# Root mean square norms of a decoder step: statistics as columns of 128 tokens, spread to rows by a product with the identity

## The chip, the cores and the metric

One core of a Trainium2 chip runs the whole step as one launch. The metric is the device time in microseconds (us), median of three runs.

## The reference

Two layers of a decoder, width 1024, over 512 prompt tokens and 8 sample tokens (520 columns, one per token). Layer 0 is a state space layer (S5), layer 1 attends with decay to a paged cache (FoX). Both attend to a memory, and each has a sandwich norm and a feed-forward part:

```python
def rmsnorm(x, g):
    y = xf * lax.rsqrt(jnp.mean(xf * xf, axis=-1, keepdims=True) + EPS)
    return y.astype(x.dtype) * g
...
        x = x + rmsnorm(o, p['norm_mix_post'][l])
        f, cp = conv_ffn(rmsnorm(x, p['norm_ffn_pre'][l]), p['w_up'][l], ...)
        x = x + rmsnorm(f, p['norm_ffn_post'][l])
```

So between two big products there are always two norms in a row: that of the product's output (post), which is added to the residual stream `x`, and that of the new `x` (pre), whose factor each token of the next product is multiplied by.

## The kernel before

Activations lie transposed: the 128 partitions are features, the 1024 features are 8 blocks `k`, and the 520 tokens are the columns, in two halves `HALF` of 264 and 256. A product runs in panels of 128 output features. A panel takes three matmuls for each `k` and half, of split operands: `x_hi` by `w_hi`, `x_lo` by `w_hi`, `x_hi` by `w_lo`. The weights' parts `w_hi` are made by ScalarE (`hi`), `w_lo` by GpSimd or VectorE (`lo`), and each stage waits for the one before by semaphores.

At four places a product is followed by two norms (`post_norm` on VectorE, `post` on ScalarE, `last_pair` and `first_pair` on TensorE): behind `wout0` (300 us), `down01` (708 us), `wout1` (1078 us), and `down11` at the end (1484 us), where only the post norm follows. The order of the work there is written out by hand, instruction by instruction, with constants that say at which step `i` or `k` something stands (`LAST_READ`, `ROOT_1`, `HI_NEXT`, `ROOT_PRE`, `RECIP_PRE`, `LO_FIRST`, `LO_NEXT`).

- `last_pair` computes the last two panels (6 and 7) by halves: half 0 of both, then half 1 of both. In the midst of half 1 of panel 6, `post_stats(stats, 0)` sums the squares of half 0 over the features: three float32 matmuls with the stationary matrix `meanw` (128x128, each entry 1/1024), so that every partition of the result holds each token's mean square. A float32 matmul is two instructions on the engine.
- ScalarE takes the root (`root_half`, 264 or 256 columns on all partitions, into `sd`), VectorE the reciprocal (`reciprocal_half`, into `rstd`).
- VectorE then goes through 16 steps (half, k): scale `y` by gain and `rstd` (L1738), add it to `x` (L1744), and two steps behind make `x_lo` (L1251). ScalarE makes `x_hi` and the squares of `x` from each new `x`. Two `w_lo` (L1208) of the next phase stand in this order too, at steps 1 and 11.
- `first_pair` computes the next phase's first two panels by halves (half 0 of both, half 1 of both), each `k` as soon as its `x_lo` is there. Behind k = 2 of its first quarter stand `post_stats(before, 1)` and the first sums of `x_stats` (`add`), one matmul with `meanw` for each block of squares; they give the pre norm's mean squares. Its reciprocals write `rstd`, by which the next phase's readers (`uc`, `qh`) multiply each panel.

The mean squares lie in a ring of four PSUM banks (`misc`), each freed by the engine that reads it.

## Time and profile before

| | |
|---|---|
| median of 3 runs | 1521.39 us (1520.93 to 1525.54) |
| span of the profiled execution | 1519.0 us |
| TensorE busy | 1413.4 us, 93% |
| VectorE busy | 976.7 us, 64% |
| ScalarE, GpSimd busy | 576.7, 638.5 us |
| mean granted TensorE clock | 0.971 |

The profile states the span from the first to the last instruction of one execution; the time of that same execution is not stated beside it. The median is 2.4 us above the span, which is what lies around it. In timelines the first two numbers are start and duration in us; PE is TensorE, DVE VectorE, ACT ScalarE, and an arrow "<-" in brackets names what ended the idle time before the instruction. Matmuls are pipelined, so that in a string of them the distance of starts, not the duration, is the cost of one.

### The profile page before, as it was taken

The numbers are of one execution on the slowest core, as the hardware profiler recorded it, in microseconds if no ns is written. First come the engines' busy times: TensorE is split into PE (matmuls) and PEld (weight loads), VectorE is DVE, ScalarE is ACT, GpSimd is POOL, SyncE is SP. The second block draws the span as 40 slices with busy tenths as digits, with TensorE's granted clock in tenths as the row PEclk, the third lists the DMA queues.
The fourth block names the chain that finished last, engine by engine and source line by source line (L and its number), as shares of the span: only waits on it lengthen the run. The fifth ranks groups of instructions, "written<-read, shape, count | busy, mean of one in ns | idle before, by whom it ended". The sixth has DMA issues, their size and how long they took to land.

```text
span 1519.0 us, 32537 instructions
## 1 busy us (share of the span) xinstructions
PE 1413.4 (93%) x12097; PEld 1313.9 (86%) x12097; DVE 976.7 (64%) x1658; ACT 576.7 (38%) x1019; POOL 638.5 (42%) x420
## 2 busy tenths in 40 slices
PE   6986978989999999999799989999989999999997
PEld 6984758979999999999699966657889999999997
DVE  5769967576773167765748688753677761376755
ACT  4544354344432133422415235432454431234323
POOL 1586422304444334433177888402223443344430
PEclk9998789989999999999999999999999999999999
DMA  5344364213333232332145769995213233233321
GB/s 173 114 117 79 63 169 123 83 44 85 99 94 98 77 97 83 102 98 75 45 121 164 226 175 308 331 340 157 69 57 97 84 103 90 83 91 88 104 83 62
DMA packets 289082, 180.47 MB, mean 119 GB/s; under 512 B 54248, under 2 KB 274572, under 8 KB 288924
## 3 DMA queue, kind: packets, MB, share of 16 engines
q1 hardware_dynamic: 288412, 179.07, 40.9%
q8 instruction: 61, 1.00, 0.3%
q14 instruction: 33, 0.27, 0.1%
q10 hardware_dynamic: 576, 0.13, 0.0%
HBM read 167.10 MB, written 10.63 MB: 117 GB/s over the span
## 4 chain that ended last, share of the span: by engine, by line
PE 70%; DVE 14%; issue 8%; ACT 2%; SPq 2%; DMA 1%; POOL 1%; DVEq 0%; ACTq 0%; POOLq 0%
PE big L2649 58%; PE big L2715 3%; PE misc L2800 2%; DVE tmp L1261 2%; PE big L2746 2%; DVE y L1738 1%; DVE rstd L1219 1%; DVE x L1744 1%; DVE w_lo L1208 1%; DVE x_lo L1251 1%; SPq L597 1%; PE misc L2770 1%; ACT yc L2506 1%; DVE cp L1261 1%; ACT w_hi L2144 1%
## 5 line engine op out<-in xcount | busy, mean ns | idle before, releaser
L949 POOL TENSOR_TENSOR w_lo<-raw,w_hi 128x1024 fp32r<-128x1024 f32 (+2 forms) x153 | 393.8, 2574 | 708.9 <-ACT w_hi L2144 548.4
L2144 ACT ACTIVATE w_hi<-raw 128x1024 fp32r<-128x1024 f32 (+2 forms) x179 | 198.5, 1109 | 582.1 <-PE big L2649 539.0
L2649 PE MATMUL big<-x_hi,w_hi 128*128 128x264 f32 x1984 | 406.7, 287 | 8.4 <-DVE uc L1827 2.8
L2649 PE MATMUL big<-x_hi,w_lo 128*128 128x264 f32 x1984 | 400.8, 283 | 0.0
L2649 PE MATMUL big<-x_lo,w_hi 128*128 128x264 f32 x1984 | 398.8, 283 | 0.0
L2649 PEld LDWEIGHTS big<-x_hi,w_hi 128*128 128x128 f32 x1984 | 305.9, 189 | 13.1 <-issue 4.7
L2649 PEld LDWEIGHTS big<-x_lo,w_hi 128*128 128x128 f32 x1984 | 305.6, 189 | 0.0
L2649 PEld LDWEIGHTS big<-x_hi,w_lo 128*128 128x128 f32 x1984 | 305.3, 189 | 0.0
L1831 DVE SCALAR_TENSOR_TENSOR yc<-uc,convw,yc 128x512 f32<-128x512 f32 x88 | 136.7, 1554 | 113.2 <-ACT yc L2506 113.2
L2649 PE MATMUL big<-h_hi,w_hi 128*128 128x264 f32 x616 | 125.1, 284 | 6.3 <-DVE h_lo L1846 6.3
L2649 PE MATMUL big<-h_hi,w_lo 128*128 128x264 f32 x616 | 123.9, 282 | 0.0
L2649 PE MATMUL big<-h_lo,w_hi 128*128 128x264 f32 x616 | 123.9, 282 | 0.0
L2649 PEld LDWEIGHTS big<-h_hi,w_hi 128*128 128x128 f32 x616 | 94.1, 188 | 7.4 <-DVE h_lo L1846 7.1
L2649 PEld LDWEIGHTS big<-h_lo,w_hi 128*128 128x128 f32 x616 | 94.4, 188 | 0.0
L2649 PEld LDWEIGHTS big<-h_hi,w_lo 128*128 128x128 f32 x616 | 94.4, 188 | 0.0
L1859 DVE COPY y<-big 128x264 f32 (+1 forms) x32 | 12.2, 424 | 102.6 <-PE big L2649 102.6
L1093 POOL TENSOR_TENSOR areas<-areas,qb 128x768 f32<-128x768 f32 x41 | 74.6, 1830 | 7.0 <-DMA areas<-in_cache_k 6.2
L1836 DVE SCALAR_TENSOR_TENSOR yc<-uc,convw,yc 128x512 f32<-128x512 f32 x88 | 66.2, 752 | 12.7 <-DVE yc L1834 0.2
L2506 ACT ACTIVATE yc<-uc,convw 128x520 f32<-128x520 f32 x88 | 72.3, 821 | 1.1
L1201 DVE TENSOR_TENSOR sumsq<-sumsq,sq 128x520 f32<-128x520 f32 x20 | 52.5, 2627 | 11.7 <-ACT sq L2461 9.9
L2746 PE MATMUL big<-x_hi,w_hi 128*128 128x264 f32 (+1 forms) x96 | 38.4, 400 | 17.8 <-DVE x_lo L1251 10.4
L1219 DVE RECIPROCAL rstd<-sd 128x264 f32<-128x264 f32 (+1 forms) x16 | 28.3, 1773 | 31.5 <-ACT sd L2177 31.5
(434 smaller groups left out, 2330.8 us busy)
## 6 DMA issues: line engine op xcount, KB each, us to landing
raw<-in_w_up SPq DMA_DIRECT2D x88, 512.0 KB, 3.9
raw<-in_w_down SPq DMA_DIRECT2D x32, 704.0 KB, 4.7
areas<-in_cache_k SPq DMA_DIRECT2D x41, 384.0 KB, 4.5
areas<-in_cache_v SPq DMA_DIRECT2D x41, 384.0 KB, 4.7
raw<-in_w_in SPq DMA_DIRECT2D x16, 512.0 KB, 4.2
raw<-in_w_out SPq DMA_DIRECT2D x16, 512.0 KB, 4.2
raw<-in_w_kv SPq DMA_DIRECT2D x12, 512.0 KB, 4.6
spare<-in_cache_k SPq DMA_DIRECT2D x12, 384.0 KB, 4.5
```

The costliest lines, as they stand in the source:

```text
L949: pool.tensor_tensor(w_lo[slot][:, 0:kb, :], raw[slot][:, 0:kb, :], w_hi[slot][:, 0:kb, :].bitcast(F32), ALU.subtract).then_inc(lo_made, 1)
L1093: own.tell(pool.tensor_tensor(p, p, qb[b % 2][:].rearrange("p (a d) -> p a d", a=2), ALU.mult), s_("k_product"), n + 1)
L1201: ins = V.tensor_tensor(sumsq[:], sumsq[:], sq[:, m % 2, :], ALU.add)
L1219: tell(V.reciprocal(rstd[:, c0:c1], sd[:, c0:c1]), s_("rstd_ready"), nstd[0])
L1261: do(V.tensor_tensor(o, a_, b_, op))
L1831: st(V.scalar_tensor_tensor(yy[:, 0:T], uu[:, 1:1 + T], w_[1], yy[:, 0:T], ALU.mult, ALU.add))
L1836: st(V.scalar_tensor_tensor(yy[:, 0:T], uu[:, 0:T], w_[0], yy[:, 0:T], ALU.mult, ALU.add))
L2144: A.activation(w_hi[slot][:, 0:kb, :], raw[slot][:, 0:kb, :], ACT.Copy).then_inc(hi_made, 1)
L2506: A.activation(yy[:], uu[:, 2:2 + NT], ACT.Identity, bias=convw[:, 1 - l, bass.ds(it + (f * KH + half * KF + 132), 1)], scale=convw[:, 1 - ...
L2649: ins = pe.matmul(big[2 * slot + b_][:, 0:c1 - c0], w[slot][:, k, :], r[:, c0:c1], start=(k == 0 and n_ == 0), stop=(k == kb - 1 and n_ == 2))
L2715: return pe.matmul(big[2 * slot + b_][:, 0:c1 - c0], w[slot][:, k, :], r[:, c0:c1], start=(k == 0 and n_ == 0), stop=(k == kb - 1 and n_ = ...
L2746: ins = pe.matmul(big[2 * slot + b_][:, 0:c1 - c0], w[slot][:, k, :], r[:, k, c0:c1], start=(k == 0 and n_ == 0), stop=(k == KD - 1 and n_ ...
```

## The change

In `post_norm`, `post`, `last_pair` and `first_pair` the statistics change their shape. The squares are now the stationary operand, 128 tokens at a time, and one column of `meanw` is the moving one. The result is a column: a token on each partition. Half 0 (264 tokens) takes three such blocks (the third overlaps the second, and only its last 8 tokens are used), half 1 (256) takes two. Root and reciprocal run on 128x3 or 128x2 elements. Then `spread_row` turns them to rows again: the reciprocals' column, repeated 128 times, is stationary and the identity moves, so that each partition of the result, in the same PSUM bank from column 8 on, holds each token's factor. VectorE reads the post norm's factors straight from there; ScalarE copies the pre norm's into `rstd`.

The constants move the roots and reciprocals to other steps, and `read_half` of panel 6 goes behind the first `y`. The norms of `x0` and of the memory stay as they were. Three start-up semaphores become one. The diff, cut:

```diff
@@ -148,6 +148,20 @@
...
+def stat_blocks(n):
+
+    c0, c1 = HALF[n]
+    full_ = [(c0 + P * j, P * j, 0) for j in range((c1 - c0) // P)]
+    over = (c1 - c0) % P
+    return full_ + ([(c1 - P, c1 - c0 - over, P - over)] if over else [])
+
+
+ROW = 8
+
+
 def by_half():
 
     return enumerate((n, k) for n in range(2) for k in range(KD))
@@ -195,8 +209,8 @@
 KV_HI = 4
-ROOT_1, HI_NEXT, ROOT_PRE, RECIP_PRE = 6, 8, 10, 13
-LO_FIRST, LO_NEXT = 1, 11
+RECIP_1, ROOT_1, HI_NEXT, ROOT_PRE, RECIP_PRE, ROWS_PRE = 7, 4, 8, 13, 15, 15
+LO_FIRST, LO_NEXT, LAST_READ_END = 1, 11, 5
 K_FIRST = (2, 3)
@@ -582,6 +596,16 @@
 
+        def stat_cols_at(i, n):
+
+            c = 8 * (i % 4)
+            w = len(stat_blocks(n))
+            return sd[:, c:c + w], sd[:, 32 + c:32 + c + w]
+
+        def stat_row(job):
+
+            return bank(job)[:, ROW:ROW + HALF[job[2]][1] - HALF[job[2]][0]]
+
         def gain(name, k, l=0):
@@ -1218,6 +1242,25 @@
 
+            ncol = [0]
+
+            def reciprocal_cols(n):
+
+                root, recip = stat_cols_at(ncol[0], n)
+                ncol[0] += 1
+                dve.wait_ge(s_("root_cols"), ncol[0])
+                tell(V.reciprocal(recip, root), s_("rstd_ready"), 3 + ncol[0])
+
+            def row_spread(i):
+
+                dve.wait_ge(s_("row_spread"), i)
+
+            def rows_read(name):
+
+                for n in range(2):
+                    _, _, read, before = place(("ms", name, n))
+                    dve.wait_ge(read, before + 1)
+
             def reciprocal_halves(name):
...
@@ -1723,24 +1766,31 @@
                 sync()
-                reciprocal_half(stats, 0)
-                sync()
-                read_half(ph, 6, 1, add)
+                last_read = LAST_READ if nxt is not None else LAST_READ_END
+                reciprocal_cols(0)
+                first = ncol[0]
+                row_spread(first)
                 steps = [k for _, k in by_half()]
...
                 for i in range(2 * KD + 2):
+                    if i == (RECIP_1 if nxt is not None else KD):
+                        reciprocal_cols(1)
                     if i == KD:
-                        reciprocal_half(stats, 1)
-                        sync()
+                        row_spread(first + 1)
                     if i < 2 * KD:
...
                         c = slice(*HALF[n])
-                        tell(V.scalar_tensor_tensor(y[:, k, c], y[:, k, c], gain(name, k, l), rstd[:, c], ALU.mult,
-                                                    ALU.mult), s_("y_scaled"), done + i + 1)
+                        tell(V.scalar_tensor_tensor(y[:, k, c], y[:, k, c], gain(name, k, l),
+                                                    stat_row(("ms", stats, n)), ALU.mult, ALU.mult),
+                             s_("y_scaled"), done + i + 1)
+                    if i == 0:
+                        read_half(ph, 6, 1, add)
                     if 1 <= i <= 2 * KD:
...
                         dve.wait_ge(s_("y_scaled"), done + i)
+                        if k == KD - 1:
+                            dve.sem_inc(place(("ms", stats, n))[2], 1)
                         tell(V.tensor_tensor(x[:, k, c], x[:, k, c], y[:, k, c], ALU.add), s_("x_updated"), done + i)
@@ -1750,14 +1800,14 @@
                         lo(PH[ph][2] + 9)
-                    if i == LAST_READ:
+                    if i == last_read:
                         read_half(ph, 7, 1, add)
...
                     if nxt is not None and i == RECIP_PRE:
-                        reciprocal_half(stat_name[1], 0)
+                        reciprocal_cols(0)
                 if nxt is not None:
-                    reciprocal_half(stat_name[1], 1)
-                    sync()
+                    reciprocal_cols(1)
+                    rows_read(stat_name[1])
 
@@ -2176,6 +2226,21 @@
 
+            ncol = [0]
+
+            def root_cols(name, n):
+
+                job, (root, _) = ("ms", name, n), stat_cols_at(ncol[0], n)
+                ncol[0] += 1
+                full(act, job)
+                tell(A.activation(root, bank(job)[:, 0:len(stat_blocks(n))], ACT.Sqrt, bias=eps[:, 0:1]),
+                     s_("root_cols"), ncol[0])
+
+            def copy_row(name, n, i):
+
+                act.wait_ge(s_("row_spread"), i)
+                freed(own, A.activation(rstd[:, slice(*HALF[n])], stat_row(("ms", name, n)), ACT.Copy), ("ms", name, n))
+
             def root_halves(name):
...
@@ -2465,7 +2530,7 @@
                 square_half(ph, 7, 0)
-                root_half(name, 0)
+                root_cols(name, 0)
                 if (ph, name) != ("down11", "d1"):
@@ -2480,14 +2545,17 @@
                         square_half(ph, 7, 1)
-                    elif i == ROOT_1:
-                        root_half(stats, 1)
-                    elif i == HI_NEXT:
+                    if i == ROOT_1:
+                        root_cols(stats, 1)
+                    if i == HI_NEXT:
                         hi(PH[after][0], base + n + 1)
-                    elif i == ROOT_PRE:
-                        root_half(name, 0)
+                    if i == ROOT_PRE:
+                        root_cols(name, 0)
+                    if i == ROWS_PRE:
+                        copy_row(name, 0, ncol[0])
+                root_cols(name, 1)
                 hi(KD, base + n + 2)
-                root_half(name, 1)
+                copy_row(name, 1, ncol[0])
                 ny[0] += 1
...
@@ -2695,11 +2763,27 @@
                     pe.wait_ge(s_("sq_used"), 2 + 6 * npost[0])
-                o, (c0, c1) = take(("ms", name, n)), HALF[n]
+                o = take(("ms", name, n))
                 pe.wait_ge(s_("sq_last"), 4 * npost[0] - 2 + 2 * n)
-                pe.matmul(o[:, 0:c1 - c0], meanw[:], sumsq[:, c0:c1], start=True, stop=False)
-                pe.matmul(o[:, 0:c1 - c0], meanw[:], sq[:, 0, c0:c1], start=False, stop=False)
-                give(pe.matmul(o[:, 0:c1 - c0], meanw[:], sq[:, 1, c0:c1], start=False, stop=True), ("ms", name, n))
+                for j, (at, _, _) in enumerate(stat_blocks(n)):
+                    t = slice(at, at + P)
+                    pe.matmul(o[:, j:j + 1], sumsq[:, t], meanw[:, 0:1], start=True, stop=False)
+                    pe.matmul(o[:, j:j + 1], sq[:, 0, t], meanw[:, 0:1], start=False, stop=False)
+                    ins = pe.matmul(o[:, j:j + 1], sq[:, 1, t], meanw[:, 0:1], start=False, stop=True)
+                give(ins, ("ms", name, n))
+
+            nrow = [0]
+
+            def spread_row(name, n):
+
+                i, o = nrow[0], bank(("ms", name, n))
+                nrow[0] += 1
+                pe.wait_ge(s_("rstd_ready"), 3 + i + 1)
+                _, recip = stat_cols_at(i, n)
+                for j, (_, at, skip) in enumerate(stat_blocks(n)):
+                    ins = pe.matmul(o[:, ROW + at:ROW + at + P - skip], recip[:, j:j + 1].to_broadcast([P, P]),
+                                    ident[:, skip:P], start=True, stop=True)
+                ins.then_inc(s_("row_spread"), 1)
 
@@ -2723,6 +2807,8 @@
                                 post_stats(stats, 0)
+                        if b_ == 1 and p_ == 0:
+                            spread_row(stats, 0)
                         if b_ == 0:
@@ -2753,6 +2839,12 @@
                                 add(b_, KD - 1)
+                            if b_ == 0 and p_ == 0 and k == 5:
+                                spread_row(before, 1)
+                            elif b_ == 1 and p_ == 0 and k == 2:
+                                spread_row(name, 0)
+                            elif b_ == 1 and p_ == 1 and k == 5:
+                                spread_row(name, 1)
                         if b_:
@@ -2763,11 +2855,12 @@
                 def add(n, k):
-                    c0, c1 = HALF[n]
                     if k == 0:
...
                     pe.wait_ge(s_("xsq_made"), done + KD * n + k + 1)
-                    ins = pe.matmul(o[n][:, 0:c1 - c0], meanw[:], y[:, k, c0:c1], start=(k == 0), stop=(k == KD - 1))
+                    for j, (at, _, _) in enumerate(stat_blocks(n)):
+                        ins = pe.matmul(o[n][:, j:j + 1], y[:, k, at:at + P], meanw[:, 0:1], start=(k == j == 0),
+                                        stop=(k == KD - 1 and at + P == HALF[n][1]))
                     if k == KD - 1:
...
@@ -3377,6 +3470,7 @@
             post_stats("d1", 1)
+            spread_row("d1", 1)
             for c, a_ in TURNED_OUT:
```

In the rows that follow, `misc` is the bank of statistics, `big` that of a panel. On TensorE, in `last_pair("wout0")`, half 1 of panel 6, before:

```order
L2715 MATMUL big<-x_lo,w_hi 128x256
L2700 MATMUL misc<-sumsq,meanw 128x264
L2701 MATMUL misc<-sq,meanw 128x264
L2702 MATMUL misc<-sq,meanw 128x264
L2715 MATMUL big<-x_hi,w_hi 128x256
L2715 MATMUL big<-x_lo,w_hi 128x256
L2715 MATMUL big<-x_hi,w_hi 128x256
```

and now, from the last three column products of the statistics on:

```order
L2770 MATMUL misc<-meanw,sumsq 128x1
L2771 MATMUL misc<-meanw,sq 128x1
L2772 MATMUL misc<-meanw,sq 128x1
L2799 MATMUL big<-x_hi,w_hi 128x256
L2799 MATMUL big<-x_lo,w_hi 128x256
L2799 MATMUL big<-x_hi,w_hi 128x256
L2799 MATMUL big<-x_lo,w_hi 128x256
L2799 MATMUL big<-x_hi,w_hi 128x256
L2799 MATMUL big<-x_lo,w_hi 128x256
L2784 MATMUL misc<-ident,sd 128x128 x2
L2784 MATMUL misc<-ident,sd 128x8
```

Three products have become nine (six of them stand ahead of these rows), and the spread of half 0 stands ahead of the panel's `w_lo` products.

On TensorE, in the `first_pair` behind it, from the post norm's statistics of half 1 (behind k = 2) on, before:

```order
L2700 MATMUL misc<-sumsq,meanw 128x256
L2701 MATMUL misc<-sq,meanw 128x256
L2702 MATMUL misc<-sq,meanw 128x256
L2770 MATMUL misc<-y,meanw 128x264 x2
L2746 MATMUL big<-x_hi,w_hi 128x264
L2746 MATMUL big<-x_lo,w_hi 128x264
L2746 MATMUL big<-x_hi,w_lo 128x264
L2770 MATMUL misc<-y,meanw 128x264
```

and now, from the first of the six statistics products on:

```order
L2770 MATMUL misc<-meanw,sumsq 128x1
L2771 MATMUL misc<-meanw,sq 128x1
L2772 MATMUL misc<-meanw,sq 128x1
L2770 MATMUL misc<-meanw,sumsq 128x1
L2771 MATMUL misc<-meanw,sq 128x1
L2772 MATMUL misc<-meanw,sq 128x1
L2862 MATMUL misc<-meanw,y 128x1 x6
L2832 MATMUL big<-x_hi,w_hi 128x264
L2832 MATMUL big<-x_lo,w_hi 128x264
L2832 MATMUL big<-x_hi,w_lo 128x264
L2862 MATMUL misc<-meanw,y 128x1 x3
```

and, behind k = 5:

```order
L2832 MATMUL big<-x_hi,w_lo 128x264
L2862 MATMUL misc<-meanw,y 128x1 x3
L2784 MATMUL misc<-ident,sd 128x128 x2
L2832 MATMUL big<-x_hi,w_hi 128x264
L2832 MATMUL big<-x_lo,w_hi 128x264
```

Each sum over a block of `x` has become three products, and the row that VectorE waits for comes from the spread (`L2784`) behind k = 5.

On VectorE, in `post_norm`, around step 8, where half 1 begins, before:

```order
L1744 TENSOR_TENSOR x<-x,y 128x264
L1251 SCALAR_TENSOR_TENSOR x_lo<-x,gains,x_hi 128x264
L1219 RECIPROCAL rstd<-sd 128x256
L1738 SCALAR_TENSOR_TENSOR y<-y,gains,rstd 128x256
L1744 TENSOR_TENSOR x<-x,y 128x264
L1251 SCALAR_TENSOR_TENSOR x_lo<-x,gains,x_hi 128x264
```

and now:

```order
L1252 RECIPROCAL sd<-sd 128x2
L1783 SCALAR_TENSOR_TENSOR y<-y,gains,misc 128x264
L1794 TENSOR_TENSOR x<-x,y 128x264
L1294 SCALAR_TENSOR_TENSOR x_lo<-x,gains,x_hi 128x264
L1783 SCALAR_TENSOR_TENSOR y<-y,gains,misc 128x256
L1794 TENSOR_TENSOR x<-x,y 128x264
```

The reciprocal of 256 columns has become one of 2, one step earlier, and the scaling reads its factors from `misc`.

## Rows read from the trace of the kernel before

**Rows 1.** The page: busy time by engine, and the chain that ended last.

```profile
PE 1413.4 (93%) x12097; PEld 1313.9 (86%) x12097; DVE 976.7 (64%) x1658; ACT 576.7 (38%) x1019; POOL 638.5 (42%) x420
...
PE 70%; DVE 14%; issue 8%; ACT 2%; SPq 2%; DMA 1%; POOL 1%; DVEq 0%; ACTq 0%; POOLq 0%
```

**Rows 2.** The page, costliest groups: the reciprocals of the norms.

```profile
L1219 DVE RECIPROCAL rstd<-sd 128x264 f32<-128x264 f32 (+1 forms) x16 | 28.3, 1773 | 31.5 <-ACT sd L2177 31.5
```

**Rows 3.** Timeline of VectorE behind `wout1`: start us, us, engine, line, what.

```profile
1089.40 0.89 DVE L1738 SCALAR_TENSOR_TENSOR y<-y,gains,rstd 128x264 f32<-128x264 f32 x2
...
1090.55 1.22 DVE L1208 TENSOR_TENSOR w_lo<-raw,w_hi 128x1024 fp32r<-128x1024 f32 x1
...
1099.99 1.75 DVE L1219 RECIPROCAL rstd<-sd 128x256 f32<-128x256 f32 x1 [0.85 <-ACT sd L2177]
1101.78 0.48 DVE L1738 SCALAR_TENSOR_TENSOR y<-y,gains,rstd 128x256 f32<-128x256 f32 x1
```

**Rows 4.** Timeline of TensorE over the same stretch.

```profile
1084.96 0.69 PE L2700 MATMUL misc<-sumsq,meanw 128*128 128x264 f32 x2
...
1095.74 0.42 PE L2746 MATMUL big<-x_hi,w_hi 128*128 128x264 f32 x1 [0.53 <-DVE x_lo L1251]
...
1096.40 1.05 PE L2700 MATMUL misc<-sumsq,meanw 128*128 128x256 f32 x2
...
1107.64 0.39 PE L2746 MATMUL big<-x_hi,w_hi 128*128 128x264 f32 x1 [2.37 <-DVE w_lo L1208]
...
1111.82 0.59 PE L2770 MATMUL misc<-y,meanw 128*128 128x256 f32 x2
...
1120.16 0.28 PE L2746 MATMUL big<-x_hi,w_lo 128*128 128x256 f32 x1
...
1121.85 0.51 PE L2649 MATMUL big<-x_hi,w_hi 128*128 128x264 f32 x2 [1.41 <-DVE uc L1827]
```

**Rows 5.** Timeline of TensorE: small matmuls with 64 or 128 stationary columns.

```profile
11.25 1.02 PE L2800 MATMUL misc<-ident,xs_tok 8*128 8x8 f32 x8
12.20 6.21 PE L2800 MATMUL misc<-ident,x_tok 128*128 128x128 f32 x32
...
949.24 0.69 PE L3032 MATMUL misc<-y,probT 128*64 128x64 f32 x16
949.85 0.83 PE L3314 MATMUL misc<-rowsel,rstd 128*128 128x2 f32 x6
950.54 0.68 PE L2998 MATMUL big<-kh,qh 128*128 128x512 f32 x1
...
1503.72 1.04 PE L2800 MATMUL misc<-ident,x 128*128 128x128 f32 x8
```

**Rows 6.** Two small operations, by line: nanoseconds min/median/max.

```profile
L1946 DVE TENSOR_TENSOR qs<-big,rstd x6: 167/168/168, 756.4 to 783.6; 128x8 f32<-128x8 f32 x6
...
L2464 ACT ACTIVATE root_warm<-eps x4: 203/203/203, 302.0 to 1486.9; 128x1 f32<-128x1 f32 x4
```

**Rows 7.** Timelines behind `down01`: VectorE, then TensorE.

```profile
722.80 1.22 DVE L1208 TENSOR_TENSOR w_lo<-raw,w_hi 128x1024 fp32r<-128x1024 f32 x1
...
756.68 0.48 PE L2649 MATMUL big<-x_hi,w_hi 128*128 128x264 f32 x2 [2.38 <-DVE qs L1946]
```

**Rows 8.** Timelines at the end: TensorE, then VectorE.

```profile
1493.41 0.61 PE L2700 MATMUL misc<-sumsq,meanw 128*128 128x264 f32 x2
...
1497.84 0.89 DVE L1738 SCALAR_TENSOR_TENSOR y<-y,gains,rstd 128x264 f32<-128x264 f32 x2
...
1507.32 0.48 DVE L1738 SCALAR_TENSOR_TENSOR y<-y,gains,rstd 128x256 f32<-128x256 f32 x1
```

**Rows 9.** Windows: busy us of PE, PEld, DVE, ACT, POOL; granted clock, DMA share, GB/s.

```profile
1096.00:1099.40 3.40, 3.40 (x11) 2.77 (x11) 3.14 (x9) 2.43 (x7) 0.00 (x0) 0.50 0.00 0
...
328.00:334.80 6.80, 6.13 (x26) 5.93 (x27) 5.03 (x10) 1.89 (x5) 0.00 (x0) 0.50 0.31 80
...
860.00:890.00 30.00, 29.38 (x233) 27.93 (x232) 26.04 (x41) 5.15 (x7) 24.33 (x13) 1.00 0.49 151
```

More of the change, by code:

```diff
@@ L148 @@
 TURNED_OUT = [(c, a) for cs in ((0, 1), (2, 3, 4)) for a in range(2) for c in cs]
+PARAMS = {"lrow": 1, "lam": 2, "gains": 3}
+def stat_blocks(n):
[4 more added lines that the diff above has]
+ROW = 8
 def by_half():
@@ L1523, in _ @@
                              dtrow[:].unsqueeze(2).to_broadcast([PAIRS, 2, STATE])))
-            mark(s_("lrow_ready"))
+            mark(s_("params_ready"))
             evac(("lam",), lam[:, 0:96], bank(("lam",))[:, 0:96])
-            mark(s_("lam_ready"))
+            mark(s_("params_ready"))
             s5_rates()
             evac(("rows",), gains[:], bank(("rows",))[:, 0:100])
-            mark(s_("gains_ready"))
+            mark(s_("params_ready"))
             evac(("xsT",), x[:, :, T:NT], bank(("xsT",))[:, 0:KD * NB].rearrange("p (k b) -> p k b", b=NB))
@@ L2223, in mem_turned @@
                 mark(s_("memtok_ready"))
-            act.wait_ge(s_("lam_ready"), 1)
+            act.wait_ge(s_("params_ready"), PARAMS["lam"])
             tell(A.activation(lam[:, 64:64 + PAIRS], lam[:, 64:64 + PAIRS], ACT.Exp), s_("s5_act"), 1)
@@ L2228, in _ @@
             do(A.activation(root_warm[:], eps[:], ACT.Sqrt))
-            act.wait_ge(s_("gains_ready"), 1)
+            act.wait_ge(s_("params_ready"), PARAMS["gains"])
             for k in range(KD):
@@ L2598, in _ @@
             square_half("down11", 7, 1)
-            root_half("d1", 1)
+            root_cols("d1", 1)
             for c, a_ in TURNED_OUT:
@@ L2802, in _ @@
             pe.wait_ge(s_("consts"), 1)
-            pe.wait_ge(s_("lrow_ready"), 1)
+            pe.wait_ge(s_("params_ready"), PARAMS["lrow"])
             pe.wait_ge(s_("lam_in"), 48)
```

## The prediction

> **What bounds the kernel now.** I read the page first: TensorE is busy 93% of the span and holds 70% of the chain that ended last, VectorE 14% [rows 1]. Where TensorE runs panels back to back a norm costs nothing, so only the four places where a product meets two norms can move the time, and they must be read one by one in the timelines of VectorE and TensorE. There the 16 reciprocals of 264 or 256 columns take 1.77 us each [rows 2]; two are those of `x0`, which stay, so 14 become small.
>
> The place behind `wout1` stands for `wout0` too. It has three links. (A) The statistics of half 0 start at 1084.96 [rows 4], the first `y` at 1089.40 [rows 3]; then `w_lo` at 1090.55 waits for what ScalarE makes once panel 6 is done. (B) TensorE takes k = 2 of the next panel at 1095.74, then the statistics of half 1 and the sums of `x` [rows 4]; VectorE waits 0.85 us for the root, spends 1.75 us on the reciprocal and starts half 1 at 1101.78 [rows 3]. (C) From there VectorE's order is fixed up to the second `w_lo`, which lets TensorE go on at 1107.64. From 1107.64 to 1120.28 (the last start plus one distance of 0.12) TensorE never waits: it, not VectorE, is the bound [rows 4]. (D) The next panel starts at 1121.85, 1.57 us later, behind the reciprocal and the first readings.
>
> So a faster VectorE helps in A, B and the tail D, while each instruction that is added on TensorE costs in B and C.
>
> **What an instruction with one moving column costs.** The trace has none, but it has its neighbours. Six float32 matmuls with 128 stationary and 2 moving columns start at 949.85 and the next matmul at 950.54: 0.115 us each; the eight with 8 moving columns go from 11.25 to 12.20: 0.119 each [rows 5]. Moving almost nothing, they cost what the stationary load costs. The lower bound is 16 matmuls with 64 stationary columns in 0.61 us, 0.038 each, so 0.076 for twice the columns if they scale [rows 5]; the upper one is 0.22 to 0.24, what a float32 instruction with 256 moving columns takes now (two between 1111.82 and the next sum about 0.79 later, of which three matmuls take 0.36: 0.43 for the pair) [rows 4]. I take 0.115, since number and shape of the stationary columns are the same. An instruction of the spread moves 128 columns as the transposes do, eight in 1.04 us, or 0.11 each [rows 5]; its block of 8 columns takes 0.115.
>
> The Trainium skill, "TensorE: Matmul & The Clock Gate", section "LDWEIGHTS (loading the stationary operand)", gives the number of columns over 1.2, so 107 ns for 128, whatever the moving side. The rows agree within 10%; by its figure the loss below would be 0.6 us smaller at each of the three places. [...]
>
> **Term A.** Statistics: 3 products with 3 blocks are 18 instructions, 2.2 us with the last one's end, where 6 took about 1.6 with it. Root and reciprocal on three columns: a 128x1 root takes 0.20 us and a 128x8 operation on VectorE 0.17 [rows 6]; I take 0.20 and 0.15 (bounds 0.06 and 0.3). TensorE has 6 panel matmuls (0.7 us) to do in the meantime, so this costs it no wait. Spread: 4 by 0.11 and 2 by 0.115, 0.83 with its end. With about 0.08 for each of four signals the first `y` starts 3.7 us behind the statistics, not 4.4: 0.7 earlier. But panel 6 ends 0.75 (18 x 0.115 less the 1.32 of now) plus 0.67 (spread) later, 1.4 us; ScalarE's `w_hi` and then `w_lo` follow it. They had about 1.2 us to spare, so the first `x_lo` comes 0.2 us **later**. Behind `down01`, where `w_lo` starts at 722.80 [rows 7] close behind its `w_hi`, 1.0 of the 1.4 is left, and the reading of panel 7 waits another 0.4: 1.4 us later.
>
> **Term B.** From k = 2 on TensorE must do: 3 matmuls (0.36), 12 instructions of statistics and 12 of the first two sums (2.76), then for k = 3, 4, 5 each 3 matmuls and 6 column instructions (3 x 1.05 = 3.15), then the spread of 4 (0.60 with its end) and a signal (0.08): 6.95 us until VectorE may start half 1. Now it is 1101.78 - 1095.74 = 6.04. VectorE's saved 1.75 + 0.85 us turn into a wait for a spread that stands three blocks further down TensorE's queue: **+0.9 us**. Root and reciprocal are hidden by those blocks; at 0.3 instead of 0.15 nothing changes.
>
> **Term C.** The stretch that TensorE bounds gets: the last sum of half 0, 6 x 0.115 against 0.44, +0.25; eight sums of half 1, 4 x 0.115 against 0.43, +0.2; the two spreads of the pre norm, 0.67 and 0.44. Together **+1.6 us**, with no cover.
>
> **Term D.** ScalarE copies the second row (a row root takes 0.48 us today, and I take that) while TensorE does its last 6 matmuls (0.71). The copy is over about when TensorE is; then come 0.37 for the `uc` start-up and 0.82 for the readings: 1.25 instead of 1.57, **-0.3**. Behind `down01` it is the same (next panel at 756.68 [rows 7]).
>
> **The end.** Statistics at 1493.41, first `y` at 1497.84; half 1 from 1507.32 [rows 8]. Half 0 starts 0.3 earlier; half 1 waits for root, reciprocal and spread behind 12 column instructions whose squares come 1.4 us later, and starts near 1506.7. From there all is as now: **-0.6**.
>
> **Sum.** `wout0` and `wout1`: 0.2 + 0.9 + 1.6 - 0.3 = 2.4 each; `down01`: 1.4 + 0.9 + 1.6 - 0.3 = 3.6; the end -0.6. Together +7.8 on a span of 1519.0, so 1526.8, and with the 2.4 that lie around it 1529.2: 1529 us, 0.5% slower.
>
> **Rivals.**
> *The load hides* (faster). If a column instruction costs no more than its share of the 64-column row, 0.038, B's 42 column instructions shrink by 3.2 us, C's 38 by 2.9. VectorE's chain then bounds B, and of its 2.6 us of wait and reciprocal about 2.3 are gained; C is paid back. With D this is near -3 us at three places, -0.6 at the end: 1512. It decides at about 0.09 us for an instruction, where B and C come to nothing. For it speaks that TensorE's loads overlap running matmuls now; against it that in both strings of small matmuls they do not get below 0.115. 0.16.
> *Half way* (within 0.3%). At 0.076, B and C shrink by 1.6 and 1.5: -0.7 at two places, +0.5, -0.6: 1520. Or the two early losses are made good while cache pages stream: but right ahead of that stage, 860 to 890 us, the DMA share is 0.49 and TensorE is busy 29.4 of 30 us [rows 9], so the stage waits for the product and starts later with it. 0.18.
> *The clock* (slower still). Behind `wout1` the granted clock was 0.50 in 1096.0 to 1099.4, just the stretch of B, and behind `wout0` 0.50 in 328.0 to 334.8, in C, where TensorE's panels took twice the time [rows 9]. Both came behind waits of TensorE of 2 us. Such waits stay, and much of the work between becomes loads; if the level stays at 1.2 GHz for one such stretch of 6.8 us more at each of three places, at some 3 us each, the time is 1538. 0.16.
> *The forecast*: 0.50.
>
> **How the numbers follow.** 0.3% (4.6 us) is about what a measurement of this kernel can tell from no change. The forecast and the clock are slower: 0.65 with the forecast's edge at +5 given to no change; half way is the same: 0.19; faster 0.16. The range reaches to the half-way case and most of the clock case, 1518 to 1537; outside lie the rest of the clock case and the hidden load.
>
> **What would show it.** Right: in strings of `128x1` matmuls starts 0.11 to 0.12 apart; VectorE idle 2 to 3 us ahead of step 8, ended by the spread; 14 to 14.5 us for the stretch from the first panel's second quarter to the end; 128x3 reciprocals under 0.2 us; the four places +2.4, +3.6, +2.4, -0.6. Wrong: starts 0.08 or less apart, or no wait ahead of step 8, or a clock at half over the whole place.

## The result

| | before | changed |
|---|---|---|
| median of 4 runs | 1523.47 us (1520.93 to 1530.24) | 1560.89 us (1557.74 to 1561.76) |
| span of the profiled execution | 1519.0 us | 1555.8 us |
| mean granted TensorE clock | 0.971 | 0.951 |

The ratio is 1.0232, 95% interval 1.0211 to 1.0254: the change costs 37 us. The forecast was 1529 with a range up to 1537, so it had the sign and missed the size by 32 us. Both profiled executions are the fastest of their four (1520.93 and 1557.74 us); where a median execution spends the 2.5 and 3.2 us more, no trace shows.

### The profile page after: what moved, and what is told of

Same layout as the page of the kernel before. It is cut to its first block, busy times and chain, and to the rows that moved or that the text cites. A ratio compares the mean times of both kernels' runs of the same rounds, so it can differ in the third digit from the quotient of the medians.

```text
span 1555.8 us, 33107 instructions
## 1 busy us (share of the span) xinstructions
PE 1458.4 (94%) x12383; PEld 1363.3 (88%) x12383; DVE 954.8 (61%) x1658; ACT 576.0 (37%) x1025; POOL 638.3 (41%) x420
## 4 chain that ended last, share of the span: by engine, by line
PE 77%; DVE 13%; issue 3%; ACT 2%; DMA 1%; SPq 1%; POOL 1%; DVEq 0%; ACTq 0%; POOLq 0%
PE big L2717 57%; PE big L2799 3%; PE big L2832 3%; PE misc L2893 2%; PE misc L2862 2%; DVE tmp L1304 2%; PE misc L3392 1%; DVE sc L1980 1%; DVE y L1783 1%; DVE w_lo L1232 1%; DVE x L1794 1%; DVE ast L1530 1%; SPq L621 1%; PE misc L3125 1%; DVE x_lo L1294 1%
## 5 line engine op out<-in xcount | busy, mean ns | idle before, releaser
L1909 DVE COPY y<-big 128x264 f32 (+1 forms) x32 | 12.2, 424 | 102.3 <-PE big L2717 102.3
L2254 ACT ACTIVATE x_hi<-x,gains 128x264 fp32r<-128x264 f32 (+2 forms) x64 | 35.3, 560 | 47.3 <-DVE x L1794 39.7
L2832 PE MATMUL big<-x_hi,w_hi 128*128 128x264 f32 (+1 forms) x96 | 38.7, 404 | 12.1 <-DVE x_lo L1294 10.5
```

Source lines behind the costliest of these rows:

```text
L2254: ins = A.activation(o, src, ACT.Copy, scale=1.0 if g is None else g)
L2832: ins = pe.matmul(big[2 * slot + b_][:, 0:c1 - c0], w[slot][:, k, :], r[:, k, c0:c1], start=(k == 0 and n_ == 0), stop=(k == KD - 1 and n_ ...
```

## The profile after

The page of the changed kernel, busy time and chain (before: [rows 1]):

```profile
PE 1458.4 (94%) x12383; PEld 1363.3 (88%) x12383; DVE 954.8 (61%) x1658; ACT 576.0 (37%) x1025; POOL 638.3 (41%) x420
...
PE 77%; DVE 13%; issue 3%; ACT 2%; DMA 1%; SPq 1%; POOL 1%; DVEq 0%; ACTq 0%; POOLq 0%
```

VectorE has become 22 us less busy, TensorE 45 us more. The costly groups, each shape by itself (busy, mean ns of one, idle time ahead):

```profile
L2862 PEld LDWEIGHTS misc<-meanw,y 128*128 128x128 f32 x240 | 46.0, 276 | 0.0
...
L1783 DVE SCALAR_TENSOR_TENSOR y<-y,gains,misc 128x256 f32<-128x256 f32 x32 | 15.1, 473 | 24.7 <-PE misc L2784 24.7
```

VectorE's idle time ahead of the reciprocals, ended by the root, was 31.5 us [rows 2] and is 43.0 ahead of the fourteen small ones (L1252). A second wait has come beside it: 24.7 us ahead of half 1's scaling, ended by the spread (L2784).

Where the 36.8 us of span went is read from windows, each from the start of half 0's statistics to the next phase's first panel (behind `wout0`, `down01`, `wout1`), and to the end. These windows are called places from here on. Columns: length, then busy time of PE, PEld, DVE, ACT and POOL, the granted clock (PEclk; 1.00 is the full 2.4 GHz, 0.50 the half), DMA share and GB/s. Before:

```profile
305.99:345.63 39.64, 32.94 (x179) 28.98 (x179) 29.44 (x60) 18.24 (x42) 2.39 (x1) 0.83 0.12 30
717.23:756.68 39.45, 30.85 (x197) 27.59 (x195) 30.67 (x62) 19.17 (x42) 3.56 (x2) 0.96 0.13 36
1084.96:1121.84 36.88, 29.18 (x180) 25.53 (x178) 29.44 (x60) 18.23 (x42) 2.40 (x1) 0.95 0.11 31
1493.41:1519.00 25.59, 16.67 (x108) 14.51 (x106) 16.32 (x36) 7.64 (x14) 0.00 (x0) 0.87 0.23 84
...
756.68:1084.96 328.28, 312.45 (x2750) 253.20 (x2751) 212.94 (x366) 119.00 (x253) 193.05 (x102) 0.99 0.70 218
```

Changed, with a stretch inside each place:

```profile
306.07:353.60 47.53, 42.15 (x265) 40.96 (x265) 23.10 (x60) 18.20 (x45) 2.36 (x1) 0.75 0.09 24
724.95:774.34 49.39, 43.69 (x282) 42.72 (x281) 24.33 (x62) 19.02 (x44) 3.07 (x2) 0.76 0.07 22
1108.37:1156.03 47.66, 42.15 (x266) 40.96 (x265) 23.13 (x60) 17.98 (x44) 2.36 (x1) 0.75 0.08 23
1527.31:1555.80 28.49, 19.27 (x136) 17.94 (x134) 13.12 (x36) 7.31 (x14) 0.00 (x0) 0.88 0.21 76
...
318.00:341.80 23.80, 21.94 (x100) 21.56 (x100) 14.20 (x37) 10.66 (x27) 0.00 (x0) 0.50 0.09 24
...
738.00:761.60 23.60, 21.74 (x100) 21.36 (x100) 14.22 (x37) 10.66 (x27) 0.00 (x0) 0.50 0.08 23
...
1120.20:1144.00 23.80, 21.94 (x100) 21.56 (x101) 14.31 (x37) 10.75 (x27) 0.00 (x0) 0.50 0.08 23
...
774.34:1108.37 334.03, 317.31 (x2751) 255.29 (x2751) 213.74 (x366) 119.19 (x253) 192.77 (x102) 0.97 0.68 215
```

The three places cost +7.9, +9.9 and +10.8, the end +2.9: 31.5 us together. The attention stage between the second and third place took 5.8 more. That is not shown to be the change's: no kernel here changes anything in that stage, and in the fourteen profiled executions it takes from 328.1 us (`post_rows`) to 334.5 (`more12`), so that it was the execution before that was short. Against the forecast's +7.8 on the span, the 36.8 are 23.7 too much in the four places and 5.8 in this stage. In each place the granted clock (from here on: the level) is at half, 1.2 GHz, for 23.6 us and more on end, though TensorE is busy 92% of that time.

The timeline of TensorE behind `wout1` (before: [rows 4]):

```profile
1108.37 0.35 PE L2770 MATMUL misc<-meanw,sumsq 128*128 128x1 f32 x2
...
1110.37 0.36 PE L2799 MATMUL big<-x_hi,w_hi 128*128 128x256 f32 x1
...
1119.39 0.39 PE L2832 MATMUL big<-x_hi,w_hi 128*128 128x264 f32 x1 [0.52 <-DVE x_lo L1294]
...
1122.10 2.70 PE L2862 MATMUL misc<-meanw,y 128*128 128x1 f32 x12
1124.66 0.57 PE L2832 MATMUL big<-x_hi,w_hi 128*128 128x264 f32 x1
...
1130.48 1.20 PE L2784 MATMUL misc<-ident,sd 128*128 128x128 f32 x4
...
1137.58 0.59 PE L2832 MATMUL big<-x_hi,w_hi 128*128 128x264 f32 x1 [0.54 <-DVE w_lo L1232]
...
1154.40 0.28 PE L2832 MATMUL big<-x_hi,w_lo 128*128 128x256 f32 x1
1156.02 0.51 PE L2717 MATMUL big<-x_hi,w_hi 128*128 128x264 f32 x2 [1.35 <-DVE uc L1877]
```

and of VectorE (before: [rows 3]):

```profile
1112.01 0.49 DVE L1783 SCALAR_TENSOR_TENSOR y<-y,gains,misc 128x264 f32<-128x264 f32 x1 [0.93 <-PE misc L2784]
...
1122.57 0.17 DVE L1252 RECIPROCAL sd<-sd 128x2 f32<-128x2 f32 x1 [0.94 <-ACT sd L2236]
...
1131.72 0.48 DVE L1783 SCALAR_TENSOR_TENSOR y<-y,gains,misc 128x256 f32<-128x256 f32 x1 [7.85 <-PE misc L2784]
```

Up to k = 2 the clock is full and everything is as forecast: 18 column instructions take 2.00 us (1108.37 to 1110.37), 0.111 each, and the first `y` starts 3.64 us behind the statistics. Then twelve take 2.56 us (1122.10 to 1124.66), **0.213 each**, VectorE waits 7.85 us where the forecast had 2 to 3, and the panels behind run at 0.22 a matmul until 1144. The fall itself, at 1120.1, is not new: it comes behind three waits of TensorE for `x_lo` (0.87, 0.92, 0.52 us), and in the kernel before the level was also down behind such waits, up to 1099.4 [rows 9]. What is new is that it stays down.

## Experiments

Two theories. **The clock**: the column products let the granted clock fall and keep it down; that is what the forecast lacks. **The count** (with the queue): the number of loads (each matmul has a load of its stationary operand, PE and PEld both x12383), and the spread's place in TensorE's queue, cost more than thought; the level is a bystander. What the runs gave, places as windows from half 0's statistics to the next panel, with their mean granted clock:

| run | median, ratio to before (95%) | `wout0` | `down01` | `wout1` |
|---|---|---|---|---|
| before | 1523 to 1525 | 39.6 (0.83) | 39.5 (0.96) | 36.9 (0.95) |
| changed | 1560.89, 1.0232 (1.0211 to 1.0254) | 47.5 (0.75) | 49.4 (0.76) | 47.7 (0.75) |
| wide64 | 1557.51, 1.0201 (1.0164 to 1.0238) | 47.6 (0.75) | 49.5 (0.76) | 46.2 (0.78) |
| wide128 | 1538.62, 1.0083 (1.0056 to 1.0110) | 42.6 (0.92) | 41.1 (1.00) | 41.0 (0.96) |
| pre_rows | 1537.74, 1.0078 (1.0048 to 1.0108) | 40.1 (0.91) | 45.0 (0.85) | 43.3 (0.84) |
| post_rows | 1534.49, 1.0069 (1.0044 to 1.0094) | 44.5 (0.73) | 42.1 (0.84) | 42.3 (0.80) |
| fill | 1549.49, 1.0159 (1.0126 to 1.0192) | 44.3 (0.81) | 47.7 (0.79) | 44.4 (0.85) |
| late_sums | 1542.90, 1.0113 (1.0068 to 1.0159) | 44.7 (0.77) | 44.8 (0.81) | 44.6 (0.77) |
| more12 | 1525.32, 0.9998 (0.9985 to 1.0012) | 38.0 (0.87) | 37.9 (1.00) | 38.0 (0.87) |
| fill_before | 1525.68, 1.0001 (0.9984 to 1.0018) | 37.7 (0.95) | 38.7 (0.96) | 37.7 (0.95) |
| more40 | 1559.01, 1.0228 (1.0208 to 1.0247) | 50.3 (0.80) | 49.6 (0.83) | 50.3 (0.80) |
| more40_wide | 1537.67, 1.0093 (1.0070 to 1.0115) | 42.6 (0.92) | 43.1 (0.96) | 42.4 (0.92) |
| late_wide | 1526.39, 1.0006 (0.9989 to 1.0023) | 37.4 (0.95) | 39.2 (0.96) | 36.2 (1.00) |
| mix | 1519.43, 0.9971 (0.9954 to 0.9987) | 36.0 (0.95) | 36.7 (1.00) | 35.1 (1.00) |

**64 moving columns for 1.** In both kinds of column product:

```diff
-ROW = 8
+ROW = 0
+WIDE, SUMS = 64, 272
...
-                    pe.matmul(o[:, j:j + 1], sumsq[:, t], meanw[:, 0:1], start=True, stop=False)
+                    pe.matmul(o[:, SUMS + WIDE * j:SUMS + WIDE * j + WIDE], sumsq[:, t], meanw[:, 0:WIDE], start=True, stop=False)
```

> The changed kernel with one difference: in the column products (statistics and sums of x) 64 equal columns of the mean matrix move instead of 1, so each takes the same stationary load but TensorE's array works through 64 columns; ScalarE takes every 64th column of the result. Clock theory (with one moving column the array does so little that the granted clock drops to 1.2 GHz and stays there for 23.9 us at each norm, and that is what costs 8 to 10 us a place): the stretches at half clock at the three norms shrink to 7 us or less, 128x64 instructions start 0.11 to 0.12 apart there, and the time is 1526 to 1535 us. Count theory (the time goes into the number of loads and the place of the spread in TensorE's queue, whatever the level): no change or slightly slower, 1560 to 1568 us. Waits theory (TensorE's waits ahead of k = 0 to 2 drop the level, not the columns): still 23.9 us at half at each place, 1560 us.

The clock theory missed: nothing changes, and each place still has 20 to 24 us at half (0.75 to 0.78 of its window). The run left the count theory and the waits standing.

**Which columns.** `pre_rows` has the old `add` of `x_stats`, with row root and row reciprocal; `post_rows` the old `post_stats` and scaling by `rstd`, with no spread between the halves. `pre_rows` on TensorE:

```diff
-                    for j, (at, _, _) in enumerate(stat_blocks(n)):
-                        ins = pe.matmul(o[n][:, j:j + 1], y[:, k, at:at + P], meanw[:, 0:1], start=(k == j == 0),
-                                        stop=(k == KD - 1 and at + P == HALF[n][1]))
+                    c0, c1 = HALF[n]
+                    ins = pe.matmul(o[n][:, 0:c1 - c0], meanw[:], y[:, k, c0:c1], start=(k == 0), stop=(k == KD - 1))
```

> The changed kernel with the sums of x (pre norms) made as rows again, root and reciprocal of 264 and 256 columns; only the post norms' statistics go through columns and the spread. 15 of the 55 column products of a place stay. Clock theory: a group of 12 instructions behind k = 2 and six panels' blocks behind it do not hold the level down; half clock 3 to 10 us a place, total 1522 to 1532. Count theory: what is lost goes by the number of column instructions, 30 of 110 and 6 of 11 spread products stay, so about a third of the 37 us is left: 1534 to 1540.

> The changed kernel with the post norms' statistics as rows again; the sums of x stay 40 column products a place, with the spread and the copies into rows behind them. VectorE has its reciprocals of 264 and 256 columns back ahead of each half, and no spread stands between the halves. Clock theory: the column sums alone keep the level at half for 15 us or more a place, total 1542 to 1560. Count theory: two thirds of the loss stay, 1545 to 1550, with the level at half no longer than before the change (3 to 7 us). The clock rows decide, not the time.

`pre_rows` ended on the count side: the level comes back sooner than in the changed kernel, but half 1's spread still stands behind k = 5, and VectorE waits 4.41 us for it at `wout0`. `post_rows` is below both ranges, with the level down for longer than before the change (0.73, 0.84 and 0.80 for 0.83, 0.96 and 0.95; at `wout0` 23.7 us on end): the sums of `x` alone do that, where VectorE waits for no spread of a post norm. So the level's length, which was to decide, is on the clock's side, and the time on neither: 10 us are lost, where the clock theory had 18 and more.

**24 column instructions into the kernel before.**

```diff
                                 add(0, 0)
                                 add(0, 1)
+                                add.more(12, 1)
...
+                def more(count, width):
+                    for _ in range(count):
+                        pe.matmul(o[0][:, 384:384 + width], meanw[:], meanw[:, 0:width], start=False, stop=False)
```

> The kernel before, with 12 column products (24 instructions, mean matrix stationary, one moving column, results unread) behind the first two sums of x at k = 2 of the first panel, at each of the three places. Count theory: 24 x 0.115 = 2.8 us, nearly all under the 2.4 us that TensorE waits for the second w_lo and the 0.4 before it: within 0.5 us a place, 1523 to 1526 us. Clock theory: the level falls to half there and stays, the panels behind take twice the time: 3 to 7 us a place, 1532 to 1545 us, with stretches at half of 10 us or more.

No loss: the 2.8 us lie in TensorE's wait for `w_lo`. A few column products cost nothing where TensorE has slack; here the count theory had the time. The level does fall behind them at `wout0`, but for 3.4 us only (0.50 in 326.4 to 329.8), and is full behind that.

**TensorE kept at work in its waits.** `fill` and `fill_before` put products of 256 moving columns into them:

```diff
+                            if b_ == 0 and p_ == 0 and k < 3:
+                                fill(slot, (7, 7, 4)[k])
                             if p_ == 0:
                                 x_split(KD * b_ + k)
```

> The changed kernel with TensorE kept at work where it waited: ahead of k = 0, 1, 2 of each first panel 7, 7 and 4 products of 256 moving columns (0.12 us each, results overwritten later) in place of waits of 0.87, 0.92 and 0.52 us, and 10 behind the spread of half 1 for the wait of 1.32. All column products stay. Clock theory (the waits let the level fall, the column products behind them keep it at half): the level stays full through k = 2 and the columns behind it, VectorE's wait ahead of step 8 is 2 to 4 us and not 7.9, and the place costs the forecast's +2.4: 1526 to 1534 us. If the columns alone bring the level down: 1545 to 1560. Count theory: 1560 to 1565, since work is only added.

> The kernel before, with TensorE kept at work in its waits as in the run above (7, 7, 4 products ahead of k = 0 to 2, and 18 ahead of the second panel, for 2.37 us). Clock theory: the half-clock stretches at wout0 (two of 6.8 us), down01 and wout1 (3.4 each) go; only C at wout0 is bound by TensorE in one of them, so about 3 us are won there and none elsewhere: 1519 to 1523 against 1524. Otherwise: 1524 to 1526, the stretches as before.

The timeline of TensorE in `fill`, behind `wout0`:

```profile
320.80 1.48 PE L2871 MATMUL misc<-meanw,y 128*128 128x1 f32 x12
322.14 0.37 PE L2840 MATMUL big<-x_hi,w_hi 128*128 128x264 f32 x1
...
322.58 0.81 PE L2871 MATMUL misc<-meanw,y 128*128 128x1 f32 x6
323.25 0.57 PE L2840 MATMUL big<-x_hi,w_hi 128*128 128x264 f32 x1
...
324.06 1.27 PE L2871 MATMUL misc<-meanw,y 128*128 128x1 f32 x6
```

and in windows:

```profile
318.50:322.80 4.30, 4.25 (x38) 4.04 (x36) 4.07 (x12) 3.38 (x10) 0.00 (x0) 1.00 0.01 3
323.10:340.00 16.90, 16.81 (x78) 16.72 (x79) 11.45 (x29) 8.20 (x20) 0.00 (x0) 0.50 0.13 34
```

With one wait of 0.15 us left ahead of them the first 24 instructions of statistics and sums run at full clock, 12 in 1.34 us (320.80 to 322.14), six more in 0.67, and then the level falls all the same, at 323, in the midst of a TensorE that has stood still for no more than that. So in the changed kernel the waits bring the fall forward and are not needed for it. In the kernel before they do matter: behind `wout1` k = 2 and the statistics now run at full level (1100.42 to 1105), where they ran at half, and the half level comes behind a wait that was not filled, 2.08 us ahead of the matmul at 1107.75. Filling won nothing there, against what the clock theory had promised: 1.0001.

**128 moving columns.** Only a line differs from `wide64`:

```diff
-WIDE, SUMS = 64, 272
+WIDE, SUMS = 128, 0
```

> As the run with 64 moving columns, with 128, as many as are loaded. With 64 the stretches at half did not shorten (23.9, 23.9, 20.5 us). If the share of time in which the array has columns to work on decides, they shorten to 7 to 14 us and the time is 1535 to 1550; if it is the stationary load in between that holds the level down whatever moves, they stay at 20 to 24 us: 1556 to 1562.

The windows of its places:

```profile
306.90:349.49 42.59, 35.51 (x266) 34.19 (x265) 23.11 (x60) 18.33 (x45) 2.36 (x1) 0.92 0.11 27
720.75:761.86 41.11, 33.80 (x282) 32.80 (x281) 24.33 (x62) 19.03 (x44) 3.08 (x2) 1.00 0.09 27
1096.12:1137.15 41.03, 33.91 (x266) 32.58 (x265) 23.13 (x60) 18.00 (x44) 2.36 (x1) 0.96 0.09 27
```

And at `wout0` from the statistics of half 1 on:

```profile
318.40:321.70 3.30, 3.30 (x20) 3.30 (x19) 2.20 (x7) 1.48 (x6) 0.00 (x0) 0.55 0.00 0
321.90:330.00 8.10, 6.78 (x57) 6.56 (x56) 4.23 (x13) 3.29 (x8) 0.00 (x0) 0.99 0.01 3
```

22 us won by moving 128 equal columns and using one. The level falls behind the same waits, but it comes back in the midst of the column products. The three places sum to 124.7 us; the forecast's terms put onto the windows before, 116.0 + 2.4 + 3.6 + 2.4, are 124.4. **With the level up for most of it, the sum comes out near the forecast's; without it the same instructions take 144.6.** That the two sums are 0.3 apart is partly luck: one by one the places are +3.0, +1.7 and +4.2, and at `wout0` 6.5 us are still at half. The median is still 9.4 above the forecast, and of the 9.3 in the spans 6.0 lie in the attention stage, where nothing was changed, and 2.7 at the end.

**The same question in the kernel before**, where no wait or shape changes: 80 added instructions that move 1 column (`add.more(40, 1)`) or 128 (`add.more(40, 128)`).

> The kernel before, with 40 column products (80 instructions, mean matrix stationary, one moving column, results unread) behind the first two sums of x at k = 2. Count theory: 80 x 0.115 = 9.2 us less the 2.8 that TensorE waits now: +6.4 a place, 1540 to 1546, levels as before. Clock theory: in 9 us with hardly a moving column the level falls and the rest of them takes 0.213 each, then the panels twice their time: +12 to +20 a place, 1560 to 1585, half clock for 15 us or more.

> The same with 128 moving columns in each of the 80 instructions. Both theories have the same loads in the same places. Clock theory: the level stays, +6.4 to +7.5 a place, 1541 to 1548, half clock 3 to 7 us a place, so 15 us or more below the run with one moving column. Count theory: the same time as that run or a little longer.

Timelines of TensorE behind `wout0`, first with one moving column:

```profile
321.37 14.25 PE L2777 MATMUL misc<-meanw 128*128 128x1 f32 x80
335.48 0.57 PE L2746 MATMUL big<-x_hi,w_hi 128*128 128x264 f32 x1
```

with the window

```profile
324.40:341.40 17.00, 17.00 (x74) 16.28 (x74) 6.34 (x15) 3.53 (x9) 0.00 (x0) 0.50 0.13 33
```

then with 128:

```profile
322.43 9.09 PE L2777 MATMUL misc<-meanw 128*128 128x128 f32 x80
331.28 0.37 PE L2746 MATMUL big<-x_hi,w_hi 128*128 128x264 f32 x1
```

The wider instructions are the faster ones, 0.111 against 0.176 on average, and 21 us of the time hang on it (1559.0 and 1537.7; intervals far apart). With one moving column the level is at half for 17.0 us on end, in which TensorE never stands still. That is the level's effect by itself. Both kernels came out below my ranges: TensorE had more slack than the 2.8 us that I took. The places with 128 columns are 4.9, 4.4 and 4.8 us longer than those of `fill_before`, of 9 us added.

**The queue.** The sums of `x` of half 0 go behind the spread, and the spread up to k = 4:

```diff
                                 post_stats(before, 1)
-                                add(0, 0)
-                                add(0, 1)
-                            elif p_ == 0 and k > (0 if b_ else LAST_READ):
+                            elif b_ == 0 and p_ == 0 and k > 4:
+                                for kk in {5: (0, 1, 2), 6: (3, 4, 5), 7: (6,)}[k]:
+                                    add(0, kk)
+                            elif b_ and p_ == 0 and k > 0:
                                 add(b_, k - 1)
```

> The changed kernel with the sums of x of half 0 put behind the spread of half 1 in TensorE's queue (three, three and one at k = 5, 6, 7) and the spread one block earlier (k = 4): 42 instructions fewer between the statistics of half 1 and their spread. Queue theory (VectorE's wait of 7.9 us ahead of step 8 is the loss): half 1 starts 5 to 8 us earlier and 4 us or more a place are won, 1545 to 1550. Clock theory: from k = 2 on TensorE at half level waits only 1.9 us in a place, so that is all there is to win whoever goes first: 1555 to 1560, the level still at half for 20 us or more.

Between half 1's statistics and the spread now stand 30 instructions of sums and three panel matmuls fewer (42 is the count of all seven sums). Both theories missed; the median is even below the queue's range, and 3 to 5 us a place are more than the waits that the clock theory counted. Half 1 starts 16.2 us behind the statistics at `wout0`, not 23.2, as the queue theory had it. But the places give back only 2.9, 4.6 and 3.1 us of the 5 to 7 by which half 1 is early: behind them TensorE at half level is the bound. So the queue is a second cause, worth about 10.5 us of the three places (of the 18 between the medians the profiled spans show 11.7, 1555.8 to 1544.1). With both edits:

> The changed kernel with both edits that helped: 128 moving columns in the column products, and the sums of x of half 0 behind the spread. Clock theory: at full level half 1 starts 14.5 to 16 us behind the statistics of half 0 (now 23.2), C keeps the forecast's +1.6, the end its +2: 1526 to 1532. Count and queue theory: the queue edit alone gave 18 us, this one the same, 1540 to 1545.

1526.4, as the clock theory had it, and no different from before. So with 128 columns the queue edit is worth 12.2 us (1538.6 to 1526.4), and clock and queue together are the whole loss. The last candidate takes from the change what pays: post norms by columns (128 moving), sums of `x` and the last norm by rows, early spread:

```diff
                         if b_ == 1 and p_ == 0 and stats != "d1":
                             spread_row(stats, 0)
...
-                            if b_ == 0 and p_ == 0 and k == 5:
+                            if b_ == 0 and p_ == 0 and k == 4:
                                 spread_row(before, 1)
-                            elif b_ == 1 and p_ == 0 and k == 2:
-                                spread_row(name, 0)
-                            elif b_ == 1 and p_ == 1 and k == 5:
-                                spread_row(name, 1)
```

> A candidate: columns (128 moving) and spread only for the post norms o0, f0, d0, o1 and f1's likes, the sums of x as rows with their row root and reciprocal as before the change, those of half 0 behind the spread of half 1, and the last norm d1 all in rows. No column product is left in C, so its +1.6 goes, and VectorE's 1.8 us of reciprocal ahead of half 1 stay away. Clock theory: places 1 to 2 us shorter than before the change where the level stays full: 1518 to 1524, against 1524. Count theory: a third of the loss, 1534 and more.

```profile
306.56:342.54 35.98, 30.81 (x208) 28.29 (x207) 26.26 (x60) 17.61 (x42) 2.40 (x1) 0.95 0.13 33
713.95:750.67 36.72, 30.89 (x225) 28.51 (x223) 27.49 (x62) 18.66 (x42) 3.56 (x2) 1.00 0.13 40
1083.95:1119.00 35.05, 29.41 (x207) 26.71 (x206) 26.24 (x60) 17.61 (x42) 2.39 (x1) 1.00 0.12 35
```

It is faster than both kernels, than the one before by little: 1519.43 against 1524.89, ratio 0.9971 (0.9954 to 0.9987).

## Why the prediction was wrong

**The price of a column instruction** held at full clock, 0.111 for 0.115. What I took for granted in the sum was that it holds at any level; at half it is 0.213.

**Term A** held: first `y` 3.64 us behind the statistics (forecast 3.7); k = 2 comes 11.02 behind them, not 10.78, so +0.24 (forecast +0.2). Behind `down01` half 1's statistics start 1.3 later (forecast +1.4 for what stands ahead of them).

**Term B is the step that failed.** From k = 2 to the start of half 1 I had 6.95 us; it took 12.33 (1119.39 to 1131.72). The work in it is the one I counted. At half level its 42 column instructions cost 0.098 more each (4.1), the nine panel matmuls of k = 3, 4, 5 about 0.1 more each (0.9), the spread 1.20 with its end for 0.60: 12.55, close to what was measured. The spread's place in the queue, behind 30 instructions of sums of `x` that nobody waits for, was in the forecast's count, but at half level each of them costs twice (`late_sums`).

**Term C** failed in the same way: from 1137.58 to the last start plus 0.12 are 16.9 us, where I had 14 to 14.5, because the level stays at half until 1144. **Term D**: 1.5 us for 1.25.

**The end** was to win 0.6 and lost 2.9. Half 1's first `y` comes 13.57 us behind the statistics (13.91 before, 13.3 forecast), so that was right in sign and half in size. But "from there all is as now" was not. The timeline of TensorE at the end, before:

```profile
1503.72 1.04 PE L2800 MATMUL misc<-ident,x 128*128 128x128 f32 x8
1508.20 1.28 PE L2800 MATMUL misc<-ident,x 128*128 128x128 f32 x8 [3.45 <-DVE x L1744]
```

and changed:

```profile
1540.64 2.77 PE L2893 MATMUL misc<-ident,x 128*128 128x128 f32 x12
1546.66 4.92 PE L2893 MATMUL misc<-ident,x 128*128 128x128 f32 x28 [3.26 <-DVEq L1793]
```

VectorE reads the factors straight from the `misc` bank and frees it only at the last `y` of half 1, so the next output transpose waits 3.26 us for a bank of the ring. With the last norm in rows the end takes 24.9 us (`post_rows`) and 25.4 (`mix`), with it in columns 27.5 to 28.5 in the other changed kernels.

**The rivals.** "The clock" named the mechanism and even the places, and was priced at 6.8 us more of half level and 3 us a place, from the two stretches that the trace of before had. It was 23.6 and more. The stretches came behind waits, and `fill_before` bears that out for the kernel before; what the rival missed is that the column products keep the level down once it has fallen (23.8 us where it was 3.4), and that in `fill` and in `more40` they lower it with hardly a wait (in `more40` at 324.4, after 3 us of them at full level). I gave it 0.16, for a change that makes 110 of the instructions of a place into loads with one column behind them. The sign of being wrong that I had named, a clock at half over the whole place, came for half of each place. The Trainium skill, "TensorE: Matmul & The Clock Gate", section "Part 1: The HAM clock gate", says that the level follows how busy TensorE has been recently; here TensorE was busy 21.94 of 23.80 us at half level, so an engine that is busy in the profile's sense need not have the full clock. "The load hides" and the first case of "half way" are refuted by the 0.111 us; the second, that the early losses are made good behind, by the 37.

What stays open: why 64 moving columns did as little as one where 128 brought the level back, and with it what about the column products keeps the level down. The runs show that they do, and that the number of moving columns decides it.

## What to carry to other kernels

When a rewrite turns a large operand into the stationary one and leaves a few columns to move, price it at both levels of TensorE's clock, and the panels behind it too. Measured here: with 80 such instructions added at each of three places a kernel took 21 us less when they moved 128 columns than when they moved one, and the changed kernel 22 us less with 128 equal columns of which one was used. And an engine that reads straight from a ring of banks holds the bank: look who takes it next.

## What the runs showed of the hardware

- A float32 instruction with a 128-column stationary operand and 1 moving column starts 0.111 us after the one before at full clock (18 in 2.00 us) and 0.213 at half (12 in 2.56 us): what sets the distance slows with the level. The same with 64 moving columns (0.111 and 0.211, `wide64`).
- A TensorE that is busy 92% of 23.8 us was granted the half clock throughout (in `more40` 17.00 of 17.00 us), and it stayed at half into the panel matmuls behind the column products.
- With 128 moving columns in the same instructions the level was full over the whole of `down01`'s place (1.00, `wide128`); in `more40_wide` 80 of them took 8.85 us (322.43 to 331.28), 0.111 each.
